# Gated-delta mixer of a two-layer diffusion step: front by tile, shorter first and last steps, halved block tables

## The reference, cut to what matters

```python
a_mat = jnp.where(strict, jnp.einsum('bhnik,bhnjk->bhnij', kb, k) * decay, 0.0)
sol = lax.linalg.triangular_solve(a_mat + jnp.eye(CHUNK), rhs, left_side=True, lower=True, unit_diagonal=True)
qk = jnp.where(causal, jnp.einsum('bhnik,bhnjk->bhnij', q, k) * decay, 0.0)
def step(S, xs):
    u = u0_c - jnp.einsum('bhck,bhkv->bhcv', w_c, S)
    o = jnp.einsum('bhck,bhkv->bhcv', qd_c, S) + jnp.einsum('bhij,bhjv->bhiv', qk_c, u)
    S = S * gt_c[..., None, None] + jnp.einsum('bhck,bhcv->bhkv', kd_c, u)
    return S, o
# context: s0 = zeros, both final states are outputs
# latents: s0 = the cached states, their final states are dropped
```

## Time and profile before

| | us |
|---|---|
| median of 3 runs (1930.94 to 1936.07) | 1931.6 |
| the profiled execution, its own time | 1930.68 |
| its span, first to last instruction | 1928.9 |
| mixer phase of layer 0 in it | about 258 to 507.6 |
| mixer phase of layer 1 in it | about 1204.7 to 1440.5 |

### The profile page before, as it was taken

The page is one execution under the profiler, slowest core; times in us unless marked ns, Lnnn a source line. Parts: engine busy times, 40 slices in busy tenths (PEclk is TensorE's granted clock), DMA queues, the critical chain, the costliest instruction groups (busy, mean ns, idle before and its releaser), DMA issues. The chain is left out here.

```text
span 1928.9 us, 33256 instructions
## 1 busy us (share of the span) xinstructions
PE 1661.5 (86%) x12165; PEld 1350.4 (70%) x12166; DVE 1217.1 (63%) x1744; ACT 936.4 (49%) x1454; POOL 259.4 (13%) x373
## 2 busy tenths in 40 slices
PE   3988887888895999999949988888989869999992
PEld 0788776777553888888838886767865458888881
DVE  1458443556544996996664882545664479999664
ACT  2244631323322886886633445322432268888651
POOL 0000036112000211111020000542110021111102
PEclk7999998999897999999969999989989879999996
DMA  8251248662304997997563110874122379999754
GB/s 333 76 200 49 99 135 242 207 196 82 118 22 175 383 412 300 376 406 274 216 223 119 46 47 1 238 210 141 45 61 119 135 301 403 402 402 404 301 199 174
DMA packets 190453, 398.75 MB, mean 207 GB/s; under 512 B 89770, under 2 KB 110274, under 8 KB 164742
## 3 DMA queue, kind: packets, MB, share of 16 engines
q1 hardware_dynamic: 164462, 329.26, 47.3%
q10 hardware_dynamic: 17384, 37.01, 4.9%
q0 software_dynamic: 8496, 30.94, 4.3%
HBM read 347.78 MB, written 49.38 MB: 206 GB/s over the span
## 5 line engine op out<-in xcount | busy, mean ns | idle before, releaser
L2320 DVE TENSOR_TENSOR expert_w_lo<-shared,expert_w_hi 128x2048 fp32r<-128x2048 f32 x192 | 433.5, 2289 | 60.7 <-ACT expert_w_hi L2259 60.7
L2259 ACT ACTIVATE expert_w_hi<-shared 128x2048 fp32r<-128x2048 f32 x192 | 366.5, 1913 | 46.9 <-PEq L146 42.1
L2186 PE MATMUL ps<-expert_w_hi,expert_x_hi 128*128 128x512 f32 x592 | 245.3, 414 | 10.1 <-DVE expert_x_lo L2315 8.8
L2188 PE MATMUL ps<-expert_w_hi,expert_x_lo 128*128 128x512 f32 x592 | 233.6, 395 | 0.0
L2187 PE MATMUL ps<-expert_w_lo,expert_x_hi 128*128 128x512 f32 x592 | 233.3, 394 | 0.0
L2186 PEld LDWEIGHTS ps<-expert_w_hi,expert_x_hi 128*128 128x128 f32 x592 | 113.5, 192 | 41.7 <-issue 13.0
L2188 PEld LDWEIGHTS ps<-expert_w_hi,expert_x_lo 128*128 128x128 f32 x592 | 112.4, 190 | 24.3
L2187 PEld LDWEIGHTS ps<-expert_w_lo,expert_x_hi 128*128 128x128 f32 x592 | 112.9, 191 | 18.8
L2156 POOL COPY expert_cur_idx<-slot_tokens 128x1 int32 x37 | 52.3, 1413 | 523.5 <-PE ps L2173 523.5
L2241 PE MATMUL ps<-expert_w_hi,expert_hid_hi 128*128 128x512 f32 x296 | 115.8, 391 | 0.5 <-ACT expert_hid_hi L2294 0.5
L2242 PE MATMUL ps<-expert_w_lo,expert_hid_hi 128*128 128x512 f32 x296 | 115.3, 390 | 0.0
(11 more groups left out here) (373 smaller groups left out, 3435.1 us busy)
## 6 DMA issues: line engine op xcount, KB each, us to landing
shared<-in_w_up SPq DMA_DIRECT2D x64, 1024.0 KB, 7.2
shared<-in_w_down SPq DMA_DIRECT2D x64, 1024.0 KB, 9.3
shared<-in_w_gate SPq DMA_DIRECT2D x64, 1024.0 KB, 8.2
qkv<-in_w_ada SPq DMA_DIRECT2D x20, 1280.0 KB, 7.0
shared<-in_w_in SPq DMA_DIRECT2D x10, 2048.0 KB, 9.2
y_table<-expert_y ACTq DMA_DIRECT2D x37, 512.0 KB, 8.4
qkvT<-in_w_ada SPq DMA_DIRECT2D x20, 768.0 KB, 8.7
setup_ada_ring<-in_w_ada SPq DMA_DIRECT2D x8, 1024.0 KB, 12.6
```

The lines of the kernel that those rows point to most:

```text
L2186: pe.matmul(bank, x_hi[:, at], w_hi[:, j, w], start=(q == 0), stop=False)
L2188: return pe.matmul(bank, x_lo[:, at], w_hi[:, j, w], start=False, stop=(q == KD - 1))
L2259: act.activation(w_hi[:, j, :], raw[:, j, :], ACT.Copy).then_inc(w_hi_done, 1)
L2320: dve.tensor_tensor(w_lo[:, j, :], raw[:, j, :], w_hi[:, j, :].bitcast(F32), ALU.subtract).then_inc(w_lo_done, 1)
```

## The change

The front works by tile: index i goes over the tiles in ORDER = 0, 1, 4, 2, 3, the keys-by-keys and keys-by-queries products are made once per tile and serve both directions; the two decay matrices of a tile are still made one each. QKF gets three buffers in turn, and the first tile's Bt, BtL and QK are written where step 0 reads them, so their stores and loads go. A main step's two directions now lie at two places of the tables, so each of bt_load, bl_load, x_load, y_load and qk_load is split by direction. In the front's SP list `base_load` moves ahead of the unit's load, and x_load(0), y_load(0) move from index 3 to right behind scatter(0) at index 2. Step 0 makes no product with the zero state, step 4 none for the last state. On PE the first pair of a main step comes behind both doubling levels instead of inside the second, and `turn` of the pair before moves into level 1. DVE and ACT follow the same order; in the last step pair 19's scores come ahead of `qku`. The tables keep only the two diagonal 64 x 64 blocks, so the zeroed area falls from 21 to 11 parts of 128 KB. `self.pairs` names the same pairs for the units as before.

```diff
@@ -48,8 +48,8 @@
 LEVELS = [16, 32]
 SB = 16
 NB = P // SB
-BASE = 2 * 4 * (P * P + P)
-BASE_PAD = 21 * P * 256
+BASE = 2 * 4 * 2 * (HB * HB + HB)
+BASE_PAD = 11 * P * 256
...
@@ -949,6 +949,8 @@
     def __init__(self, ph, G, A, l):
         self.G, self.A, self.l = G, A, l
         self.todo = [(l, u) for u in range(4, self.NU)] + [(l + 1, u) for u in range(4) if l + 1 < DEPTH]
+        self.pairs = list(range(1, len(self.todo) + 1))
...
+    ORDER = [0, 1, NT - 1, 2, NT - 2]
...
-        QKF = M.o[:, 2:4, :].rearrange("p t (h n) -> p t h n", h=DH)
-        BtF = [M.o[:, t, :].rearrange("p (d h n) -> p d h n", d=2, h=DH) for t in (1, NT - 1)]
-        BtLF = [M.aT[:, j, 3 * P:5 * P].rearrange("p (h n) -> p h n", h=DH) for j in (2, 3)]
+        BtF = [Bt] + [M.o[:, t, :].rearrange("p (d h n) -> p d h n", d=2, h=DH) for t in (1, NT - 1, 1, NT - 1)]
+        BtLF = [BtL] + [M.aT[:, j, 3 * P:5 * P].rearrange("p (h n) -> p h n", h=DH) for j in (2, 3, 2, 3)]
+        QKF = [QK] + [a for i in range(2) for a in (M.o[:, 2:4, :].rearrange("p t (h n) -> p t h n", h=DH), z)]
...
+        def place(s, d):
+
+            return ORDER.index(tiles(s)[d])
...
-            of = table[s * BASE:(s + 1) * BASE].rearrange("(e x) -> e x", x=P * P + P)[:, 0:P * P]
-            return of.rearrange("e (r n) -> r e n", n=P)[half(b), :, half(b)]
+            of = table[s * BASE:(s + 1) * BASE].rearrange("(e c x) -> e c x", c=2, x=HB * HB + HB)[:, b, 0:HB * HB]
+            return of.rearrange("e (r n) -> r e n", n=HB)
...
+                def front_out(i):
+                    sp.wait_ge(s_["b_done"], at(i, 1))
                     for b in range(2):
-                        sp.dma_start(large(A.base_b, s, b), eight_of(BtF[s % 2], b)).then_inc(s_["bt_out"], 16)
-                    sp.wait_ge(s_["bl_done"], at(s, 1))
-                    sp.dma_start(A.corner[s], flat(BtLF[s % 2])).then_inc(s_["bl_out"], 16)
-
-                def base_load(s):
-                    sp.wait_ge(s_["bt_out"], 32 * (s + 1))
-                    if s == 3:
+                        sp.dma_start(large(A.base_b, i, b), eight_of(BtF[i], b)).then_inc(s_["bt_out"], 16)
+                    if i:
+                        sp.wait_ge(s_["bl_done"], at(i, 1))
+                        sp.dma_start(A.corner[i], flat(BtLF[i])).then_inc(s_["bl_out"], 16)
+
+                def base_load(i):
+                    sp.wait_ge(s_["bt_out"], 32 * (i + 1))
+                    if i == 3:
                         sp.wait_ge(s_["inv_done"], 1)
-                    sp.dma_start(V[rows_of(s), 0], small(A.base_b, s, 0)).then_inc(base_in[group(s)], 16)
-                    sp.dma_start(W[rows_of(s)], small(A.base_b, s, 1)).then_inc(base_in[group(s)], 16)
-                    sp.wait_ge(s_["bl_out"], 16 * (s + 1))
-
-                def qk_store(s):
-                    sp.wait_ge(s_["qk_done"], at(s, 1))
-                    sp.dma_start(A.qk_table[s], QKF.rearrange("p d h n -> p (d h n)")).then_inc(s_["qk_out"], 16)
+                    sp.dma_start(V[rows_of(i), 0], small(A.base_b, i, 0)).then_inc(base_in[group(i)], 16)
+                    sp.dma_start(W[rows_of(i)], small(A.base_b, i, 1)).then_inc(base_in[group(i)], 16)
+                    if i:
+                        sp.wait_ge(s_["bl_out"], 16 * i)
...
                 def bt_load(s):
-                    if s:
-                        sp.wait_ge(s_["nt_done"], lev(s - 1, LV - 1, 1))
-                    for b in range(2):
-                        sp.dma_start(eight_of(Bt, b), large(A.base_b, s, b)).then_inc(s_["bt_in"], 16)
+                    sp.wait_ge(s_["nt_done"], lev(s - 1, LV - 1, 1))
+                    for d in range(2):
+                        for b in range(2):
+                            sp.dma_start(Bt[half(b), d], large(A.base_b, place(s, d), b)[:, d * DH:(d + 1) * DH]).then_inc(s_["bt_in"], 16)
...
+                def scatter(i):
+                    sp.wait_ge(s_["inv_done"], group(i) + 1)
+                    p = rows_of(i)
+                    for d in range(2):
+                        sp.dma_start(small(A.base_x, i, d), (Rt if d else R)[p, d]).then_inc(base_out[group(i)], 16)
+                        sp.dma_start(small(A.base_y, i, d), (R if d else Rt)[p, d]).then_inc(base_out[group(i)], 16)
...
+                            sp.dma_start(X[half(b), d], large(A.base_x, place(s, d), b)[:, d * DH:(d + 1) * DH]).then_inc(s_["xy_in"], 16)
...
-                for s in range(FRONT):
-                    qk_store(s)
-                    if s + 1 < FRONT:
-                        front_out(s + 1)
-                    units.load_after(sp, s)
-                    if s + 1 < FRONT:
-                        base_load(s + 1)
-                    if s == 1:
-                        bt_load(0)
-                        bl_load(0)
-                        qk_load(0)
-                    if s == 2:
+                for i in range(FRONT):
+                    if i:
+                        qk_store(i)
+                    if i + 1 < FRONT:
+                        front_out(i + 1)
+                        base_load(i + 1)
+                    units.load_after(sp, i)
+                    if i == 2:
                         scatter(0)
-                    if s == 3:
                         x_load(0)
                         y_load(0)
-                    units.store_after(sp, s)
+                    units.store_after(sp, i)
...
                 inverses(0)
+                masked(0)
+                pool.wait_ge(s_["nt_done"], lev(0, LV - 1, 1))
                 inverses(1)
-                masked(0)
-                kept(0)
-                pool.wait_ge(s_["sg_done"], 2)
                 inverses(2)
...
+                def gram(i):
+                    if i:
+                        pe.wait_ge(s_["bl_done"], at(i - 1, 1))
+                    four(2, keys(ORDER[i]), keys(ORDER[i]), "g_p")
+
+                def crossed(i):
+                    if i:
+                        pe.wait_ge(s_["qk_done"], at(i - 1, 1))
+                    four(3, keys(ORDER[i]), queries(ORDER[i]), "kq_p")
...
-                for s in range(FRONT):
-                    for d, t in enumerate(tiles(s)):
-                        pe.wait_ge(s_["bl_done"], at(s, d))
-                        four(2 + d, keys(t), queries(t), "kq_p")
-                    if s + 1 < FRONT:
-                        decays(s + 1)
-                    if s:
-                        turn(s - 1)
-                    if s + 1 < FRONT:
-                        gram(s + 1)
-                    next_scores(s)
+                crossed(0)
+                for i in range(FRONT):
+                    if i + 1 < FRONT:
+                        decays(i + 1)
+                    if i:
+                        turn(i - 1)
+                    if i + 1 < FRONT:
+                        gram(i + 1)
+                        crossed(i + 1)
+                    next_scores(i)
...
-                                pe.wait_ge(s_["xy_in"], 64 * (s + 1))
+                                pe.wait_ge(s_["xy_in"], 128 * (s + 1))
                                 if s:
                                     pe.wait_ge(s_["o_done"], at(s - 1, d))
                                 else:
                                     pe.wait_ge(s_["e_done"], at(FRONT - 1, d))
                             eight(d, 0, lambda h: NTb[:, v, d, h, :], lambda h: X[:, d, h, :], "t1_p")
-                        if v == 1:
-                            next_scores(m)
+                        if v:
+                            turn(m - 1)
...
                             eight(2 + d, 0, lambda h: T1[:, d, h, :], lambda h: Y[:, d, h, :], "yy_p")
-                        if v == 0:
-                            turn(m - 1)
-                    if s == 0:
-                        pe.wait_ge(s_["s_zero"], 1)
-                    if s == 1:
-                        pe.wait_ge(s_["s_in"], 16)
+                    next_scores(m)
                     pe.wait_ge(s_["x_done"], lev(s, LV - 1, 0))
-                    four(0, kT[0], lambda h: S[:, st, 0, h, :], "ks_p")
+                    if s:
+                        if s == 1:
+                            pe.wait_ge(s_["s_in"], 16)
+                        four(0, kT[0], lambda h: S[:, 1, 0, h, :], "ks_p")
...
                     next_scores(m + 1)
                     for d in range(2):
-                        pe.wait_ge(s_["z_done"], at(s, d))
-                        four(d, lambda h: YF[:, d, h, :], lambda h: z[:, d, h, :], "xz_p")
-                    for d in range(2):
-                        pe.wait_ge(s_["u2_done"], at(s, d))
-                        pe.wait_ge(s_["oz_done"], at(s, d))
-                        four(2 + d, lambda h: M.krow[:, tt[d], h * P:(h + 1) * P], lambda h: u2[:, d, h, :], "ds_p")
+                        if s:
+                            pe.wait_ge(s_["z_done"], later(s, d))
+                        else:
+                            pe.wait_ge(s_["yo_done"], 1)
```

(8 more changed lines are left out.)

238 lines of the change are left out of this document (130 added, 108 removed).

## The result

The changed kernel takes 1941.25 us in the median of 5 runs (1940.21 to 1946.02), the kernel before 1932.33 in the runs beside it. The ratio is 1.005, 95% interval 1.0033 to 1.0067, so it is slower by about 9.7 us. The forecast was 1943.0 and its range 1922 to 1953. The profiled execution of the changed kernel took 1940.9 us with a span of 1939.2, against 1930.7 and 1928.9 before.

What follows compares the result with a forecast made beforehand. DMA and its queue bound the kernel while units last, PE and its partners afterwards. Projection -7.4, layer 0 +12.3 and layer 1 +7.4 total +12.3, added to the profiled 1930.7 us: 1943.0, range 1922 to 1953.

Steps and rivals of the forecast that it cites:

- The projection: Layer 0's projection: smaller zeroing of base_x and base_y no longer holds ACT long; -7.4 us.
- under 1 us: Sign expected in the changed profile: ACT's second zeroing in layer 0 issues in under 1 us, taken at about 0.6.
- SP, load 3: Front, SP's list: load 3 follows scatter, X and Y, 21.2 us behind load 2; +5.2 layer 0, +7.3 layer 1.
- Unit 0 sooner: Front of layer 0: unit 0's products come after four fours less, 2.5 us earlier; 0 taken in layer 1.
- SP, loads 6 and 9: Main steps: fourteen DMAs ahead of the load instead of seven, +3.7 us each; layer 0 both, layer 1 only load 6.
- Units behind the levels: First pairs of steps 0, 1, 2: xx and yy products now precede units; +1.0 unit 4, +1.3 units 7 and 10.
- Behind the last unit: After the last unit: earlier products, -1.1 layer 0, -2.1 layer 1; shorter main steps, -2.8 and -3.8 us.
- the steps behind the units: Main steps 3 and 4 in layer 0, 2 to 4 in layer 1: shorter, -2.8 and -3.8 us.
- the extra issues are free: Rival: additional DMA issues ahead of loads 6 and 9 cost nothing; about 1932 us, chance 0.20.
- x_load's wait is absorbed: Faster rival: scatter's landing and X and Y issues fit before unit 2's products end; about 1918 us, chance 0.16.
- ACT is still held as before: Rival, layer 0's projection: second zeroing holds ACT as before, +7.4; about 1950 us, chance 0.04.
- Removed products cost nothing to keep: Front's ten fours per layer, 9.8 us, and some 6 us in steps 0 and 4, costed at nothing except before unit 0.

## Why the prediction was right, and where its sizes were off

**The projection: -7.4, measured -7.25** (load 0 at 252.25 instead of 259.50), and 8.3 alone. The mechanism had a step that failed: the second zeroing was to take "about 0.6" us to issue, and took 4.45, which by the prediction's own sign ("under 1 us") makes the term's reason wrong. The sum was right because the price had been read from layer 1, where nothing is held, and the 4.45 fit under PE's work.

**SP, load 3: +7.7 and +7.3 in time behind load 2; measured 9.1 and 7.4** (22.6 and 21.25 us apart). By parts: scatter 7.25 (7.3), its landing 3.5 (3.0), X and Y 5.3 (4.8), stores of the unit and QK 1.6 (1.6), the front's stores 2.2 (1.9), their landing 1.8 (1.7), V and W 1.0 (0.9). Every part is there; those that came out short most are the scatter's landing and the eight issues, at 0.66 instead of 0.6, by 0.5 us each. The run with X and Y back shows the largest term that the change added: 16.6 us over the two layers, against 13.3 for the split loads at three places.

**Unit 0 sooner by 2.5 in layer 0.** Its products were sooner by 3.9, as the four removed fours alone give (268.88 behind load 0 at 252.25 is 16.63, before 20.55). But load 1 was only 2.2 sooner, because base_load(2) now stands ahead of it and SP came 3.3 us after the products, where it had come 1.7 after them. A cost that I had left out, the new wait on the front's store, came to about what I had put down for DVE. The run with base_load back shows it.

**SP, loads 6 and 9: +3.7 each; measured +4.95, +5.2 and, in layer 1, +4.5.** Mis-sized: I took 0.53 us per issue "as the halved DMAs have half the descriptors". Half the size does not make the issue shorter; it is 0.65 us for 64x4x64 as for 64x8x64. Seven times that and a little is the 5. The run with split loads alone shows the term by itself.

**Units behind the levels: +1.0, +1.3, +1.3, layer 1 +1.0, +1.3.** Too high. From load 3 to load 5 layer 0 lost 0.7 and layer 1 won 1.9; from load 6 to load 8 layer 0 lost 0.1; from 9 to 11 it won 2.1. By the run with the pair back in level 1, its unit is 0.3 to 0.9 late where a load waits for it, and the one before it is multiplied sooner. Some part of that is a load that lands faster: load 9 to unit 9 took 8.45 us, and 9.60 before; that the small DMAs no longer run beside it is argued, not shown.

**Behind the last unit: -3.9 in layer 0 from load 11 on, measured -3.8; -4.6 in layer 1 from load 7 on, measured -4.5.** These sums agree by luck. They run to the tail's second group, and 1.0 and 2.3 us of them are the tail's first group at a higher granted clock, which nothing in the prediction's reasoning gives. Up to the tail the steps won 2.9 and 2.2 us. The terms were too large by 1.0 and 2.4; step 3 itself is only 0.5 us shorter (30.05 against 30.57), not 1.0.

**The sum** was +12.3 in layer 0 and +7.4 in layer 1. Up to the tail layer 0 came out at +13.3, with errors that cancel: the way to loads 3, 6 and 9 dearer by 5 us, the units' places cheaper by as much, the steps behind the units worth 1.0 less. Layer 1 came out at +5.5, 1.9 less than forecast: loads 1 and 2 came 1.3 sooner where I had taken 0, and from load 3 to 5 it won 1.9 instead of losing 1.0; against that stand 0.9 for loads 3 and 6 and 1.5 from load 6 on. That the measured time lies within 2 us of 1943.0 is thus luck in part: several terms were off by 1 to 3 us in both directions, and the clock in the tail gave back 3.3. (The 1943.0 itself adds the +12.3 to the profiled execution of 1930.7; from the median of 1931.6 it would be 1943.9.)

**The rivals.** That the extra issues are free fell with the split loads. That x_load's wait is absorbed fell with X and Y back. That ACT is still held as before fell with the small tables. The measured value is also 0.5% off, more than the 0.3% set as the bound of "no change", on the side on which the forecast put it.

**Removed products cost nothing to keep.** That was the claim on which everything else hung, and for the front's products the doubled ones bear it out: twenty fours more for 1.4 us, give or take 5.

## What to carry to other kernels

When a single-buffered load chain sets the time, count what stands ahead of each of its issues in the queue's list, issues and waits alike: a DMA issued one line earlier delays the chain by its issue time, 0.65 us here for 64x4x64 as for 64x8x64, and by the landing of whatever it waits for. The same kind of issue takes longer right behind a fresh 2,048 KB load: one 32x16x16 store took 3.50 us there in the kernel before (at 337.10) and 0.49 a few issues later. Work removed elsewhere mostly lengthened the wait for the chain; loosening the chain itself took one list of pair numbers here and was worth 55 to 59 us. Measure an order again after such a step, since the order that won 47 us under the pressed chain lost 17 to 21 without it.

## What the runs showed that was not expected

- A DMA of half the size takes as long to issue: 2.60 us for four of 64x4x64, 1.31 for two of 64x8x64, in the changed kernel and in the split loads alone.
- The second zeroing on ACT holds it for 4.45 us with 1,408 KB ahead of it and 10.32 with 2,688 KB; the time grows by 5.9 us for 1,280 KB, but none of the runs tells what the bound is.
- The tail phase's first six products take 2.81 to 5.46 us in these kernels with no change to them. Where they were 5.14 and 2.81 us the granted clock was 0.54 and 1.00, after the same 1.53 us of idle time. That is up to 2.6 us, as large as a term of the sum; why the clock was at its upper level in one execution and not in the other is open.
- Moving one pair on PE alone, with ACT's and DVE's order unchanged, cost 24 us by the ratios, 5.3 us in main step 3, with no engine at its limit.
